# Matrix products that take their columns as two halves in turns, eight columns at a time

## The chip, the cores and the metric

One Trainium2 chip, one of its cores. The time is the device time of one execution of the program in microseconds (us); lower is better. TensorE (PE in the profile) does the matrix products, with its weight loads shown apart as PEld; VectorE (DVE), ScalarE (ACT) and GpSimd (POOL) do the rest, and the SyncE queue (SP) issues the DMAs.

## The reference, cut to what matters

A trunk of two layers on 512 tokens of width 1024, all in float32: a Mamba-2 mixer, a gated MLP, a differential attention mixer, a second gated MLP. The work of interest is that of the big projections, each a product of tokens with a weight matrix:

```python
proj = jnp.einsum('bsd,de->bse', u, w_in)            # 1024 -> 6176, SSM mixer
... jnp.einsum('bse,ed->bsd', y.astype(u.dtype), w_out)   # 2048 -> 1024
qkv = jnp.einsum('bsd,de->bse', u, w_qkv)            # 1024 -> 3072, attention
... jnp.einsum('bse,ed->bsd', out.reshape(b, s, H * ATTN_V_DIM), w_out)  # 1024 -> 1024
h = jnp.einsum('bsd,df->bsf', u, w_up)               # 1024 -> 5632, both MLPs
return jnp.einsum('bsf,fd->bsd', jax.nn.silu(gate) * up, w_down)   # 2816 -> 1024
```

Between them stand RMS norms, short causal convolutions, the chunked state-space recurrence and the attention of 8 heads.

## The kernel before

Activations lie transposed: 128 channels on the partitions, the 512 tokens in the free dimension. A projection is cut into weight units of 8 (or 11) tiles of 128x128. For each unit a DMA brings the float32 weights into `raw`; ScalarE rounds them to fp32r in `w_hi` (L416), VectorE takes the remainder into `w_lo` (L431). The activations are split in the same way into `hn_hi`/`hn_lo`, `y_hi`/`y_lo`, `h_hi`/`h_lo` and `o_hi`/`o_lo`.

The helper `product` (L464 to L470) then issues three fp32r matmuls for each pair of a weight tile and an activation chunk: high weights by high activations (L468), high by low (L469), low by high (L470). All three add into the same PSUM accumulator of 512 columns by 128 partitions, and every matmul is preceded by the load of its own weight tile. The activations are the moving operand: their columns, the tokens, pass through the array one after another. Each operand of `product` is one contiguous stretch of float32 columns along a partition, and so is the accumulator that is written.

`product` is called from `in_unit` (one accumulator of 512 columns for 8 chunks), `first_unit`, `out_halves_pe`, `sout_start`, `aout_step`, and, at the boundaries between phases, from `pair_pe` and `wide_start` with the tokens cut into two parts of 256 columns (`tokens(t)`), so that norms of the first part can start while the second is multiplied. Counted over the program that is 1600 products on 512 columns and 464 on 256 columns, three matmuls each.

All other matmuls are issued elsewhere: float32 products of the recurrence and of the attention (L1080, L1083, L1092, L1111, L1597, L1647), transposes (L1104, L1119, L1607, L1640), norm statistics and broadcasts (L489, L523, L525, L529, L603, L607, L614). Between the units stand waits of the TensorE queue on semaphores (`lo_made` for the weights, `evac` for a free accumulator). The order of all queues is written out by hand in one block per engine. Nothing in the program looks at the order in which the columns of one accumulator were written: VectorE and ScalarE take an accumulator (L1050, for example) only when `unit_done` says that its last matmul has ended.

In the allocation of the program before, the tiles that are moved begin at multiples of 32 bytes in a partition (`hn_lo` at 69984, `hn_hi` at 86368, `h_hi` at 102752, for example), and each accumulator at the start of a PSUM bank of 2048 bytes or 1024 bytes into one.

Of the kernel before, what the change touches and what calls it, by code (L numbers as in the profile page):

```python
# [35 lines left out]
FC = DFF // P  # L36
HU = FC // 2
UW = HU * P
EPS = 1e-6
LAMBDA_INIT = 0.8 - 0.6 * math.exp(-0.3 * 1)  # L40
MASKED = -1e30
# [26 lines left out]
def phases():  # L68
    made, prev = [], None
    for units, chunks, width, kind in (  # L70
            (1 + 6 * NG, 1 + 6 * NG, KC * P, "in"), (2 * KC, KC, KC * P, "out"),
            (2 * FC, 2 * FC, KC * P, "in"), (2 * KC, KC, UW, "out"),
            (3 * NH, 3 * NH, KC * P, "in"), (KC, KC, KC * P, "out"),
            (2 * FC, 2 * FC, KC * P, "in"), (2 * KC, KC, UW, "out")):
        prev = Phase(units, chunks, width, kind, prev)
# [28 lines left out]
def trunk(nc, x_in, w_mix, w_sout, w_up0, w_dn0, w_qkv, w_aout, w_up1, w_dn1, params, lam_in, out):  # L104
    ctx = ExitStack()
    with ctx:
# [4 lines left out]
        def sb(name, shape, dt=F32, scope=ctx):  # L111
            return scope.enter_context(nc.sbuf_tensor(name, shape, dt))
# [4 lines left out]
        x = sb("x", [P, KC, S])  # L117
        raw = sb("raw", [P, 2, UW])
        sb("lead_in", [P, 56])
        w_hi = sb("w_hi", [P, 2, UW], F32R)  # L120
        w_lo = sb("w_lo", [P, 2, UW], F32R)
        sb("lead_out", [P, 72])
# [177 lines left out]
        norm_no, n = {}, 0  # L300
# [155 lines left out]
        def wait_up_bank(pe, ph, j):  # L456
# [4 lines left out]
            else:  # L461
                pe.wait_ge(evac["in"], ph.before["in"] + j - 3)

        def product(acc, slot, c, hi, lo, first, last, weights=None):  # L464

            wh, wl = weights or (w_hi[:, slot, :], w_lo[:, slot, :])
            wh, wl = wh[:, c * P:(c + 1) * P], wl[:, c * P:(c + 1) * P]
            nc.tensor.matmul(acc[:], wh, hi, start=first, stop=False)  # L468
            nc.tensor.matmul(acc[:], wh, lo, start=False, stop=False)  # L469
            return nc.tensor.matmul(acc[:], wl, hi, start=False, stop=last)  # L470

        def in_unit(pe, ph, j, rep):

            pe.wait_ge(lo_made, ph.U0 + j + 1)
            if ph in (UP0, UP1):
                wait_up_bank(pe, ph, j)
                acc = up_acc(ph, rep)
            else:
                wait_bank(pe, ph, j)
                acc = acc_of(ph, rep)  # L480
            for c in range(KC):
                last = product(acc, slot_of(ph, rep), c, hn_hi[:, c, :], hn_lo[:, c, :],
                               c == 0, c == KC - 1)
            last.then_inc(unit_done, 1)
# [79 lines left out]
        def first_unit(pe, j, mid=None):  # L564

            pe.wait_ge(lo_made, j + 1)
            if j in (3, 5, 7):
                pe.wait_ge(evac["in"], {3: 2, 5: 3, 7: 4}[j])
            for c in range(KC):
                last = product(mix_acc(j), slot_of(MIX, j), c, hn_hi[:, c, :], hn_lo[:, c, :], c == 0, c == KC - 1,  # L570
                               halves_of(MIX, j, True))
                if mid is not None and c == mid[0]:
                    mid[1]()
            last.then_inc(unit_done, 1)
# [43 lines left out]
        def pair_pe(pe, ph, b, hi, lo, tiles):  # L618
# [4 lines left out]
            if ph is not AOUT:  # L623
                k0 = tiles
                for s in range(2):
                    u = ph.units - 4 + s
                    pe.wait_ge(lo_made, made_at(ph, u))
                    wait_bank(pe, ph, 2 * END + s)
                    for c in range(tiles):
                        for t in range(2):  # L630
                            last = product(part_acc(ph, t, s), slot_of(ph, u), c, hi[:, c, tokens(t)],
                                           lo[:, c, tokens(t)], c == 0, False)
                    last.then_inc(unit_done, 1)
# [1272 lines left out]
        def _(pool):  # L1906
            n = 0

            def const(ins):
                nonlocal n  # L1910
                ins.then_inc(consts, 1)
                n += 1
# [8 lines left out]
            const(nc.gpsimd.memset(ones[:], 1.0))  # L1921
            const(nc.gpsimd.memset(eps[:], EPS))
            for i, width in enumerate((D, DI // NG, 2 * DH)):
# [241 lines left out]
```

## Time and profile before

| | |
|---|---|
| median of 3 runs | 1435.64 us (1434.94 to 1436.01) |
| profiled execution, device time | 1436.27 us |
| its span, first to last instruction | 1434.5 us |
| PE busy | 1417.3 us, 99% |
| PEld busy | 1192.6 us, 83% |
| DVE busy | 1027.8 us, 72% |
| ACT busy | 621.3 us, 43% |
| POOL busy | 112.9 us, 8% |
| granted TensorE clock, mean | 0.998 of full speed |

The busy time of an engine is the union of the spans of its instructions. Matmul spans overlap each other, since a second one enters the array while the first still drains, so the length of one matmul in the profile (389 ns for 512 columns) is a latency; what a stream of them costs is read from the distance between their starts.

### The profile page before, as it was taken

To read this page: it belongs to the slowest core of one execution; us is meant where nothing else is said; L and a number is where in the kernel's file an instruction comes from. 1 tells how busy PE (TensorE), PEld (TensorE's weight loads), DVE (VectorE), ACT (ScalarE), POOL (GpSimd) and SP (SyncE) were. 2 spreads that over 40 slices of the span, in tenths; PEclk is the share of its full clock that TensorE was granted. 3 is DMA by queue.
4 is the path that set the end of the run, shared out by engine and by line. 5 is a ranking of instruction groups with operands and counts; after the bars stand their busy time and mean duration, and the time that the engine had idled before them with its cause. 6 is when DMAs were issued, how large, how long until landed. Compare 5 with 4: busy or idle time off the path is not lost.

```text
span 1434.5 us, 21763 instructions
## 1 busy us (share of the span) xinstructions
PE 1417.3 (99%) x7506; PEld 1192.6 (83%) x7506; DVE 1027.8 (72%) x1575; ACT 621.3 (43%) x1019; POOL 112.9 (8%) x85
## 2 busy tenths in 40 slices
PE   8999999999999999999999999999999999999997
PEld 6888888888889888888888977777798888888887
DVE  6998889899437888888623677778588888886123
ACT  6656555557334323323323446556563332323221
POOL 0000000000110000000011032321110000000111
PEclk9999999999999999999999999999999999999999
DMA  4433332432231232323233112121212222233331
GB/s 169 176 137 126 142 125 109 138 140 74 89 132 38 96 102 88 102 91 110 101 101 139 31 59 74 59 74 56 89 63 84 92 102 96 94 105 103 101 101 60
DMA packets 37445, 142.34 MB, mean 99 GB/s; under 512 B 4176, under 2 KB 6352, under 8 KB 35344
## 3 DMA queue, kind: packets, MB, share of 16 engines
q1 hardware_dynamic: 37392, 141.63, 28.8%
q8 instruction: 34, 0.56, 0.2%
q14 instruction: 19, 0.16, 0.0%
HBM read 139.38 MB, written 2.23 MB: 99 GB/s over the span
## 4 chain that ended last, share of the span: by engine, by line
PE 94%; DVE 3%; DMA 1%; ACT 1%; issue 1%; SPq 0%; POOL 0%; POOLq 0%; ACTq 0%
PE bank L468 20%; PE bank L470 20%; PE bank L469 20%; PE b_x L468 7%; PE b_x L470 7%; PE b_x L469 7%; PE b_norm L1647 1%; PE b_norm L489 1%; PE b_y L1080 1%; PE b_y L468 1%; PE b_y L470 1%; PE b_y L469 1%; PE b_cb L1607 1%; DVE hn_lo L823 1%; PE b_x L1092 1%; PE b_y L1597 1%
## 5 line engine op out<-in xcount | busy, mean ns | idle before, releaser
L416 ACT ACTIVATE w_hi<-raw 128x1024 fp32r<-128x1024 f32 (+1 forms) x201 | 222.9, 1109 | 406.3 <-PE bank L470 291.1
L431 DVE TENSOR_TENSOR w_lo<-raw,w_hi 128x1024 fp32r<-128x1024 f32 (+1 forms) x181 | 234.1, 1293 | 229.2 <-ACT w_hi L416 229.1
L468 PE MATMUL bank<-hn_hi,w_hi 128*128 128x512 f32 x848 | 335.9, 396 | 2.9 <-DVE hn_lo L804 1.6
L470 PE MATMUL bank<-hn_hi,w_lo 128*128 128x512 f32 x848 | 330.8, 390 | 0.0
L469 PE MATMUL bank<-hn_lo,w_hi 128*128 128x512 f32 x848 | 330.3, 389 | 0.0
L468 PEld LDWEIGHTS bank<-hn_hi,w_hi 128*128 128x128 f32 x848 | 159.3, 188 | 38.1 <-DVE w_lo L431 3.2
L470 PEld LDWEIGHTS bank<-hn_hi,w_lo 128*128 128x128 f32 x848 | 159.2, 188 | 33.9
L469 PEld LDWEIGHTS bank<-hn_lo,w_hi 128*128 128x128 f32 x848 | 159.4, 188 | 32.1
L468 PE MATMUL bank<-h_hi,w_hi 128*128 128x512 f32 (+1 forms) x352 | 127.9, 363 | 0.0
L470 PE MATMUL bank<-h_hi,w_lo 128*128 128x512 f32 (+1 forms) x352 | 127.6, 362 | 0.0
L469 PE MATMUL bank<-h_lo,w_hi 128*128 128x512 f32 (+1 forms) x352 | 127.6, 362 | 0.0
L468 PE MATMUL b_x<-hn_hi,w_hi 128*128 128x512 f32 x320 | 124.6, 389 | 0.0
L469 PE MATMUL b_x<-hn_lo,w_hi 128*128 128x512 f32 x320 | 124.5, 389 | 0.0
L470 PE MATMUL b_x<-hn_hi,w_lo 128*128 128x512 f32 x320 | 124.5, 389 | 0.0
L1064 DVE SCALAR_TENSOR_TENSOR cv_s<-ug_s,par,cv_s 128x512 f32<-128x512 f32 x96 | 72.0, 750 | 6.9 <-DVE cv_s L1064 0.9
L469 PEld LDWEIGHTS bank<-h_lo,w_hi 128*128 128x128 f32 x352 | 66.4, 189 | 10.3
L470 PEld LDWEIGHTS bank<-h_hi,w_lo 128*128 128x128 f32 x352 | 66.4, 189 | 10.3
L468 PEld LDWEIGHTS bank<-h_hi,w_hi 128*128 128x128 f32 x352 | 66.4, 189 | 10.3
L1498 ACT ACTIVATE sg<-cg 128x512 f32<-128x512 f32 x44 | 27.9, 633 | 104.3 <-DVE cg L1064 104.3
L468 PEld LDWEIGHTS b_x<-hn_hi,w_hi 128*128 128x128 f32 x320 | 60.1, 188 | 13.0 <-issue 0.6
L469 PEld LDWEIGHTS b_x<-hn_lo,w_hi 128*128 128x128 f32 x320 | 60.1, 188 | 12.5
L470 PEld LDWEIGHTS b_x<-hn_hi,w_lo 128*128 128x128 f32 x320 | 60.1, 188 | 12.5
(326 smaller groups left out, 2476.7 us busy)
## 6 DMA issues: line engine op xcount, KB each, us to landing
raw<-w_up SPq DMA_DIRECT2D x80, 512.0 KB, 3.2
raw<-w_mix SPq DMA_DIRECT2D x48, 512.0 KB, 3.3
raw<-w_dn SPq DMA_DIRECT2D x32, 704.0 KB, 4.1
raw<-w_qkv SPq DMA_DIRECT2D x20, 512.0 KB, 3.2
acs_bc<-scratch SPq DMA_DIRECT2D x8, 1024.0 KB, 5.7
ecs_bc<-scratch SPq DMA_DIRECT2D x8, 1024.0 KB, 4.7
raw<-w_sout SPq DMA_DIRECT2D x16, 512.0 KB, 3.2
first_raw<-w_up SPq DMA_DIRECT2D x8, 512.0 KB, 6.4
```

Of the source, the lines that this page charges most:

```text
L416: nc.scalar.activation(halves_of(ph, j if own else rep, own or first and j < 4)[0], raw_of(ph, rep, first and j < 4), ACT.Copy).then_inc(h ...
L431: nc.vector.tensor_tensor(lo, raw_of(ph, rep, first), hi.bitcast(F32), ALU.subtract).then_inc(lo_made, 1)
L468: nc.tensor.matmul(acc[:], wh, hi, start=first, stop=False)
L469: nc.tensor.matmul(acc[:], wh, lo, start=False, stop=False)
L470: return nc.tensor.matmul(acc[:], wl, hi, start=False, stop=last)
L489: last = nc.tensor.matmul(b_norm[:, b:b + 1], squares[:, b * P:(b + 1) * P], mean_col[:, mean:mean + 1], start=True, stop=True)
L823: nc.vector.scalar_tensor_tensor(hn_lo[:, m, tokens(t)], x[:, m, tokens(t)], gain(*GAINS[b][1], m), hn_hi[:, m, tokens(t)].bitcast(F32), A ...
L1064: ins = nc.vector.scalar_tensor_tensor(dst, ug[:, t:t + S], col(wcol + t), dst, ALU.mult, ALU.add)
L1080: last = nc.tensor.matmul(dst, xdt[:, c, hh, :], m_t[:, hh, c * P:(c + 1) * P], start=True, stop=c == 0)
L1092: last = nc.tensor.matmul(b_x[:, c // 2, (c % 2) * 2 * P:(c % 2) * 2 * P + 2 * P], btok[:, c, :], xdd[:, c, :, :].rearrange("p h d -> p (h ...
L1498: nc.scalar.activation(sg[:], cg[:], ACT.Silu).then_inc(gate_ready, 1)
L1597: last = nc.tensor.matmul(scores_in[i % 2][:, t, 0:keys], qT[DH * t:DH * t + DH, b1, i * P:(i + 1) * P], kT[DH * t:DH * t + DH, b1, 0:keys ...
```

## The change

`product` gives every operand of its three matmuls another order. `in_turns` splits the columns into two halves (h = 2), and each half into runs of 8 columns (i = 8), and walks run 0 of the first half, run 0 of the second, run 1 of the first, and so on. For 512 columns this is 0 to 7, 256 to 263, 8 to 15, 264 to 271, up to 504 to 511; for the products on 256 columns the two halves are 128 apart. A run is 32 bytes; the next run begins 1024 bytes further on (512 for 256 columns), and the one after that 992 bytes back (480). The accumulator is written in the same order as the moving operand is read, so that every sum lands where it did before. The weight loads, the waits, the queues and all other matmuls stay as they are.

```diff
+RUN = 8
...
+        def in_turns(columns):
+
+            return columns.rearrange("p (h n i) -> p n h i", h=2, i=RUN)
+
         def product(acc, slot, c, hi, lo, first, last, weights=None):
 
             wh, wl = weights or (w_hi[:, slot, :], w_lo[:, slot, :])
             wh, wl = wh[:, c * P:(c + 1) * P], wl[:, c * P:(c + 1) * P]
-            nc.tensor.matmul(acc[:], wh, hi, start=first, stop=False)
-            nc.tensor.matmul(acc[:], wh, lo, start=False, stop=False)
-            return nc.tensor.matmul(acc[:], wl, hi, start=False, stop=last)
+            acc, hi, lo = in_turns(acc), in_turns(hi), in_turns(lo)
+            nc.tensor.matmul(acc, wh, hi, start=first, stop=False)
+            nc.tensor.matmul(acc, wh, lo, start=False, stop=False)
+            return nc.tensor.matmul(acc, wl, hi, start=False, stop=last)
```

## Rows read from the trace of the kernel before

**Rows 1.** Page: span, busy time and share of each engine, granted clock by slices, chain

```profile
span 1434.5 us, 21763 instructions
...
PE 1417.3 (99%) x7506; PEld 1192.6 (83%) x7506; DVE 1027.8 (72%) x1575; ACT 621.3 (43%) x1019; POOL 112.9 (8%) x85
...
PEclk9999999999999999999999999999999999999999
...
PE 94%; DVE 3%; DMA 1%; ACT 1%; issue 1%; SPq 0%; POOL 0%; POOLq 0%; ACTq 0%
```

**Rows 2.** Waits of PE: who waited, for whom, us in total, times, longest

```profile
PE b_cb L558 <- POOL last_row L1916: 3.2, 1, 3.2
PE bank L468 <- DVE hn_lo L804: 1.6, 1, 1.6
PE bank L468 <- DVE w_lo L431: 1.0, 1, 1.0
PE b_cb L1607 <- ACT aT L1691: 0.9, 2, 0.5
```

**Rows 3.** Groups by line and shape: line, tiles, shapes, count, busy us, mean ns

```profile
L468 PE MATMUL bank<-hn_hi,w_hi 128*128 128x512 f32 x848 | 335.9, 396 | 2.9 <-DVE hn_lo L804 1.6 <-DVE w_lo L431 1.0 <-issue 0.2
...
L468 PE MATMUL b_x<-hn_hi,w_hi 128*128 128x512 f32 x320 | 124.6, 389 | 0.0
...
L468 PE MATMUL bank<-h_hi,w_hi 128*128 128x512 f32 x264 | 102.7, 389 | 0.0
...
L468 PE MATMUL bank<-h_hi,w_hi 128*128 128x256 f32 x88 | 25.2, 287 | 0.0
...
L1092 PE MATMUL b_x<-xdd,btok 128*128 128x256 f32 x48 | 11.8, 381 | 0.6 <-DVE xdd L1436 0.6
```

**Rows 4.** Timeline of PE, FFN stage, 512 columns: start us, length us, what

```profile
599.87 0.39 PE L468 MATMUL bank<-hn_hi,w_hi 128*128 128x512 f32 x1
...
600.10 0.39 PE L469 MATMUL bank<-hn_lo,w_hi 128*128 128x512 f32 x1
...
600.33 0.39 PE L470 MATMUL bank<-hn_hi,w_lo 128*128 128x512 f32 x1
...
601.91 0.39 PE L468 MATMUL bank<-hn_hi,w_hi 128*128 128x512 f32 x1
```

**Rows 5.** Timeline of PE at 256 columns, end of the mixer's output projection

```profile
430.78 0.28 PE L468 MATMUL b_x<-y_hi,w_hi 128*128 128x256 f32 x1
...
432.94 0.28 PE L468 MATMUL b_x<-y_hi,w_hi 128*128 128x256 f32 x1
```

**Rows 6.** Timeline of PE from a float32 product into a unit of fp32r products

```profile
102.28 1.46 PE L1092 MATMUL b_x<-xdd,btok 128*128 128x256 f32 x6
...
103.80 0.40 PE L469 MATMUL bank<-hn_lo,w_hi 128*128 128x512 f32 x1
...
105.88 0.39 PE L469 MATMUL bank<-hn_lo,w_hi 128*128 128x512 f32 x1
...
108.83 0.39 PE L470 MATMUL bank<-hn_hi,w_lo 128*128 128x512 f32 x1
```

**Rows 7.** DVE groups by shape: a plain read of PSUM, and one in runs of 64

```profile
L1050 DVE TENSOR_TENSOR ug_f<-bank,r_pre 128x512 f32<-128x512 f32 x40 | 27.5, 687 | 0.0
...
L1436 DVE TENSOR_TENSOR xdt<-b_x,dt_tok 128x512 f32<-128x512 f32 x16 | 10.2, 682 | 0.7 <-PE b_x L1104 0.7
```

**Rows 8.** Stretches: PE, PEld, DVE, ACT, POOL busy us (instructions), clock, DMA share, GB/s

```profile
500.00:750.00 250.00, 250.00 (x1105) 207.01 (x1104) 176.91 (x232) 75.59 (x90) 8.13 (x4) 1.00 0.29 97
1100.00:1290.00 190.00, 190.00 (x840) 157.39 (x839) 157.44 (x214) 57.76 (x71) 0.00 (x0) 1.00 0.29 98
```

## Prediction, made before the change was run

> **What bounds the kernel now.** I read the page first: PE is busy for 99% of the span, the chain that ended last lies on PE for 94%, and the granted clock is full in all 40 slices, that is 2.4 GHz [rows 1]. The waits of PE come to some ten microseconds in all, most of them at the start; the four longest are shown [rows 2]. Then the stretches: over 250 us and over 190 us of the two MLPs PE is never idle, while VectorE is busy for 71% and 83% of the time [rows 8]. So the time is what TensorE's own stream takes. The busy share doesn't say how well that stream runs, since the matmuls overlap. For that I took the distance between starts from the timeline. At 512 columns nine steps lie between 599.87 and 601.91, 226.7 ns each [rows 4]. At 256 columns eighteen steps lie between 430.78 and 432.94, 120.0 ns each [rows 5]. The difference, 106.7 ns for 256 columns, is 0.4167 ns for a column: one column in each cycle of 2.4 GHz. What is left is 13.3 ns for each matmul, whatever its length. So the stream already moves a column in every cycle, and there is no slack under it: whatever the new order costs a column is paid in full.
>
> **How much work the change touches.** Of the 1600 products on 512 columns the largest groups of L468 show 848, 320 and 264; of the 464 on 256 columns the largest shows 88 [rows 3]; the rest follows from the loops. With three matmuls each that is 4800 matmuls of 226.7 ns, 1088.2 us, and 1392 of 120.0 ns, 167.0 us: 1255 us, 87% of the span of 1434.5. They move 4800 x 512 + 1392 x 256 = 2.814 million columns, 1172.5 us at 0.4167 ns, and hold 6192 x 13.3 ns = 82.6 us of the fixed part. In the new order a matmul of 512 columns has 64 runs and 63 jumps between them, one of 256 has 32 runs and 31 jumps: 4800 x 63 + 1392 x 31 = 345,552 jumps.
>
> **Part by part.** The change adds no instruction, no wait and no transfer, and moves none. The weight loads keep their contiguous operand. The number of columns is the same. Three things could have a price.
>
> 1. The jumps of the addresses, on the reading side (SBUF) and on the writing side (PSUM). No matmul in this trace reads or writes in short runs, so the price has to be bounded. The lower end is nothing; below it the stream can't go, as it moves a column in every cycle of the full clock already [rows 1, 4, 5]. Only the fixed part could shrink, and that is a rival below. The nearest rows for a broken pattern are VectorE's: reading PSUM in runs of 64 columns, each with a factor of its own, takes 682 ns for 512 elements, where a plain read of an accumulator takes 687 [rows 7]. That row is no cheap proof, as VectorE moves an element only every 1.3 ns by it and its runs are longer. The upper end is a row of PE itself: float32 products (L1092) have starts (1.46 - 0.38) / 5 = 216 ns apart at 256 columns [rows 6], with 0.38 us as the length of one [rows 3]. That is 0.84 ns for a column, half the rate of fp32r. If the new order were read or written at that rate, 1172.5 us would become some 2345 us or more.
>
> I take nothing. The start of each run lies on a multiple of 32 bytes, since the tiles do and the jumps are multiples of 32; a run therefore fills whole aligned groups of 2, 4 and 8 columns on both sides, and whatever unit up to 32 bytes the memories work in, the number of units touched for a matmul is what it was. Only a unit above 32 bytes, or a stop at every jump, would make it cost.
>
> The page "PSUM — Partial Sum Buffer" of the Trainium skill (section Specifications) speaks against this: it says that any access pattern that isn't contiguous slows matmuls significantly, its lines being 8 bytes. It gives no figure; by it the sum would end anywhere between my estimate and the half-rate case. The page "Advanced Engine Details and Errata" (section Memory Cachelines) says the same and then narrows it: every two consecutive elements should be contiguous, and in SBUF a line of 16 bytes should be hit at least twice. By that reading runs of eight cost nothing. No row here decides between the two.
>
> 2. The set-up of a pattern with three dimensions rather than one, once for each of 6192 matmuls. What a set-up that isn't hidden looks like is seen behind the float32 products: the nine steps from 103.80 to 105.88 take 231.1 ns, the thirteen from 105.88 to 108.83 take 226.9 [rows 6]. So 4.2 ns is the price of a stream whose preparation runs late, and 6192 x 4.2 = 26 us would be the upper end. I take 0: the next matmul's set-up has 120 ns or more of the running one to hide behind [rows 5], and if that cover were gone it is this 26 us that would show.
>
> 3. The readers of the accumulators. They start on `unit_done`, attached to the last matmul, which ends when all columns are written in either order. Cost 0; their cover is the next unit's 24 matmuls, 5.4 us.
>
> **The sum.** The profiled execution took 1436.27 us, span 1434.5 and 1.8 around it. Plus 0 for each part: 1436.3 for such an execution, and 1435.6 as the median, since the profiled one lay 0.6 above it.
>
> **The rivals.**
>
> *A stop at each jump (slower).* If the address generator, the SBUF read or the PSUM write loses one column time at every jump, 345,552 x 0.4167 ns = 144 us come on top: 1580 us. At two column times, one cycle of a 1.2 GHz side, it is 288 us: 1724 us. The place is inside each matmul; it decides from the first cycle lost, since nothing hides it [rows 8]. For it: the stream has no slack at all, one column in every cycle [rows 4, 5]. Against it: aligned runs of eight leave time to fetch ahead. The rule in the PSUM page would be met by this. Chance 10% for one, 7% for two column times.
>
> *Half rate or worse (slower).* If a memory is used in units above 32 bytes, each run wastes the other half of its unit, and the stream goes at the 0.84 ns for a column of the float32 products [rows 6]: 1172.5 us more, some 2610 us. Chance 10%.
>
> *Unhidden set-up (slower).* Part 2 at its upper end: 1462 us; at a fifth of it 5 us, still to be measured. Chance 6%.
>
> *A smaller fixed part (faster).* The 13.3 ns between the columns of two matmuls might depend on where the last column of one and the first of the next lie; the new order ends still at the last column and starts at the first, so I see no reason for it. All of it gone would give 1436 - 83 = 1353 us; a tenth of it is 8 us, 1427 us. Chance 3%.
>
> *The change does not do what it says.* If the order is folded back into a plain one, the time is that of the forecast; this lies in its 64%, and only the experiments behind the result could tell it apart.
>
> **How the numbers follow.** A measurement of this kernel can tell a difference of 0.2%, 2.9 us, from no change. No change 64%, slower 10 + 7 + 10 + 6 = 33%, faster 3%. The likeliest case's own range is 1433 to 1439. The whole range runs from 1433 over the unhidden set-up up to one column time at each jump, 1582: 64 + 6 + 10 = 80%. Two column times, half rate and a gain are left out.
>
> **What would show it.** Right: starts still 226.7 ns apart at 512 columns and 120.0 at 256, in the same stretches; the length of one matmul still 389 and some 287 ns [rows 3]; span within 3 us. A stop at each jump shows as 226.7 + 26.3 = 253 ns and 120.0 + 12.9 = 133 ns (279 and 146 for two), so that the part over 13.3 ns grows with the columns; half rate as some 440 ns; an unhidden set-up as the same few nanoseconds at 512 and at 256. VectorE's and ScalarE's groups shouldn't change in length in any case; in the slow ones they only wait longer for PE. The prediction is wrong if the step at 512 columns moves by more than 0.5 ns.

## The result, and the profile after

The changed kernel takes 1514.56 us (1514.48 to 1516.09, 4 runs) where the kernel before takes 1435.61 (1434.94 to 1436.01): 79 us more, a ratio of 1.0553 with a 95% interval of 1.0535 to 1.0571. The forecast was no change.

| | before | after |
|---|---|---|
| span of the profiled execution | 1434.5 us | 1512.8 us |
| PE busy | 1417.3 us | 1497.6 us |
| PEld busy | 1192.6 us | 1206.9 us |
| DVE busy | 1027.8 us | 1029.4 us |
| ACT busy | 621.3 us | 621.2 us |
| granted TensorE clock, mean | 0.998 | 0.998 |

From the page of the kernel after, the lines that answer to [rows 1]:

```profile
span 1512.8 us, 21763 instructions
...
PE 1497.6 (99%) x7506; PEld 1206.9 (80%) x7506; DVE 1029.4 (68%) x1575; ACT 621.2 (41%) x1019; POOL 111.0 (7%) x85
...
PEclk9999999999999999999999999999999999999999
...
PE 98%; DMA 0%; ACT 0%; DVE 0%; issue 0%; SPq 0%; POOL 0%; POOLq 0%; ACTq 0%
```

The number of instructions is the same, the granted clock is full throughout, which is 2.4 GHz, and VectorE and ScalarE do the same work in the same time. PE has grown by 80 us, and the weight loads (PEld), which overlap it, by 14. PE's waits are as small as before, the largest again the 3.2 us at the start. So the time must lie between the starts of matmuls. The timeline of PE in the same stage as [rows 4], 512 columns:

```profile
639.93 0.40 PE L474 MATMUL bank<-hn_hi,w_hi 128*128 128x512 f32 x1
...
640.17 0.41 PE L475 MATMUL bank<-hn_lo,w_hi 128*128 128x512 f32 x1
...
640.42 0.40 PE L476 MATMUL bank<-hn_hi,w_lo 128*128 128x512 f32 x1
...
642.85 0.40 PE L474 MATMUL b_x<-hn_hi,w_hi 128*128 128x512 f32 x1
```

Twelve steps lie between 639.93 and 642.85: 243.3 ns each, where [rows 4] gave 226.7. At 256 columns (to be read beside [rows 5]) 33 steps lie between these two rows, 123.3 ns each by the unrounded starts, where there were 120.0:

```profile
824.83 0.28 PE L475 MATMUL b_x<-h_lo,w_hi 128*128 128x256 f32 x1
...
828.89 0.29 PE L475 MATMUL bank<-h_lo,w_hi 128*128 128x256 f32 x1
```

4800 x 16.6 + 1392 x 3.3 ns = 84 us; the span grew by 78. Most of the rest is in two places. In the stages with other matmuls between the units of products, a step was up to 231 ns long before the change already [rows 6], and the first seven steps behind such matmuls grew by 11 to 13 ns only. And three stretches of 114 matmuls at 256 columns, one at the head of each projection that follows a boundary between phases, last 14.2 us before and 14.3 after. TensorE waits there for VectorE's splits into `hn_lo`, of which one comes every 1.58 us where twelve matmuls take 1.44 before and 1.48 after, so that a longer step only means less waiting. The groups by shape say the same from another side (they answer to [rows 3]):

```profile
L474 PE MATMUL b_x<-hn_hi,w_hi 128*128 128x512 f32 x320 | 129.8, 406 | 0.0
...
L474 PE MATMUL bank<-h_hi,w_hi 128*128 128x512 f32 x264 | 107.1, 406 | 0.0
...
L474 PE MATMUL bank<-h_hi,w_hi 128*128 128x256 f32 x88 | 25.4, 289 | 0.0
```

One matmul of 512 columns lasts 406 ns in place of 389, 17 more: as much as the step. The time is lost inside the stream of columns, and five times as much at 512 columns as at 256, though there are only twice as many runs. A fixed price for each jump would have given 2 to 1.

For the rest of this document a "step" is the distance between the starts of two matmuls in a stage of one kind, in ns; "at 512" is read from a stretch of 40 us in the middle of the first MLP, "at 256" from its last units. It holds for that stretch; in some orders the same products have another step elsewhere, which is said where it was read. One column time is 0.4167 ns.

### The profile page after: what moved, and what is told of

Same layout as the page of the kernel before. It is cut to its first block, busy times and chain, and to the rows that moved or that the text cites. A ratio compares the mean times of both kernels' runs of the same rounds, so it can differ in the third digit from the quotient of the medians.

```text
span 1512.8 us, 21763 instructions
## 1 busy us (share of the span) xinstructions
PE 1497.6 (99%) x7506; PEld 1206.9 (80%) x7506; DVE 1029.4 (68%) x1575; ACT 621.2 (41%) x1019; POOL 111.0 (7%) x85
## 4 chain that ended last, share of the span: by engine, by line
PE 98%; DMA 0%; ACT 0%; DVE 0%; issue 0%; SPq 0%; POOL 0%; POOLq 0%; ACTq 0%
PE bank L474 21%; PE bank L475 20%; PE bank L476 20%; PE b_x L474 8%; PE b_x L476 8%; PE b_x L475 8%; PE b_y L474 1%; PE b_y L476 1%; PE b_y L475 1%; PE b_norm L1653 1%; PE b_norm L495 1%; PE b_y L1086 1%; PE b_cb L1613 1%; PE b_y L1603 1%; PE b_y L1089 1%; PE b_x L1098 1%
## 5 line engine op out<-in xcount | busy, mean ns | idle before, releaser
L474 PE MATMUL bank<-hn_hi,w_hi 128*128 128x512 f32 x848 | 349.4, 412 | 2.5 <-DVE hn_lo L810 1.2
L476 PE MATMUL bank<-hn_hi,w_lo 128*128 128x512 f32 x848 | 344.5, 406 | 0.0
L475 PE MATMUL bank<-hn_lo,w_hi 128*128 128x512 f32 x848 | 344.4, 406 | 0.0
L474 PE MATMUL bank<-h_hi,w_hi 128*128 128x512 f32 (+1 forms) x352 | 132.5, 376 | 0.0
L475 PE MATMUL bank<-h_lo,w_hi 128*128 128x512 f32 (+1 forms) x352 | 132.3, 376 | 0.0
L476 PE MATMUL bank<-h_hi,w_lo 128*128 128x512 f32 (+1 forms) x352 | 132.2, 376 | 0.0
L474 PE MATMUL b_x<-hn_hi,w_hi 128*128 128x512 f32 x320 | 129.8, 406 | 0.0
L476 PE MATMUL b_x<-hn_hi,w_lo 128*128 128x512 f32 x320 | 129.8, 406 | 0.0
L475 PE MATMUL b_x<-hn_lo,w_hi 128*128 128x512 f32 x320 | 129.8, 406 | 0.0
L474 PEld LDWEIGHTS bank<-h_hi,w_hi 128*128 128x128 f32 x352 | 66.8, 190 | 14.2
L476 PEld LDWEIGHTS bank<-h_hi,w_lo 128*128 128x128 f32 x352 | 66.8, 190 | 14.2
L475 PEld LDWEIGHTS bank<-h_lo,w_hi 128*128 128x128 f32 x352 | 66.7, 189 | 14.3
```

The lines of the kernel that those rows point to most:

```text
L474: nc.tensor.matmul(acc, wh, hi, start=first, stop=False)
L475: nc.tensor.matmul(acc, wh, lo, start=False, stop=False)
L476: return nc.tensor.matmul(acc, wl, hi, start=False, stop=last)
```

## The experiments

### Which side pays, and is it a price for each run?

Four kernels: two other lengths of a run, and the turns on one side only.

```diff
-RUN = 8
+RUN = 16
```

> Runs of 16 columns in place of 8: 32 runs in a matmul of 512 columns, 16 in one of 256. Before the change the starts of matmuls of 512 and 256 columns lay 226.7 and 120.0 ns apart, after it 243.3 and 123.3. Theory A: each run costs one column time (0.4167 ns), and some 10 ns of this vanish in the fixed part of 13.3 ns, so that a step is the larger of (columns + 32) and (columns + runs + 8) column times: 552, 230.0 ns, at 512 and 288, 120.0 ns, at 256. 4800 x 3.3 ns = 16 us, some 1451 us. Theory B: nothing vanishes, the price of a jump depends on its distance, 16.7 / 63 = 0.264 ns at 1024 bytes and 3.3 / 31 = 0.107 ns at 512 bytes: 31 x 0.264 = 8.2 ns at 512 columns, 234.9 ns, and 121.6 ns at 256: some 1474 us.

Measured: 1496.2 us, ratio 1.0417 (1.0399 to 1.0434); steps 240.0 and 120.0 ns. At 256 columns as theory A had it, at 512 columns not: the price is 13.3 ns, where A says 3.3 and B 8.2. Halving the number of runs took away only a fifth of the price of 16.6.

```diff
-RUN = 8
+RUN = 4
```

> Runs of 4 columns: 128 runs in a matmul of 512 columns, 64 in one of 256. Theory A (step = larger of columns + 32 and columns + runs + 8, in column times): 648, 270.0 ns, at 512 and 328, 136.7 ns, at 256; 4800 x 43.3 + 1392 x 16.7 ns = 231 us by the steps, and since the change itself cost 79 us where its steps give 85, some 1650 us. Theory B (0.264 ns for a jump of 1024 bytes, 0.107 for one of 512, nothing vanishes): 260.2 ns and 126.7 ns, some 1595 us. Theory C: a memory works in units of 32 bytes, and half a unit costs as much as a whole one: 1024 columns' time for 512, above 430 ns a step, some 2500 us.

Measured: 1550.8 us, ratio 1.0796 (1.0778 to 1.0814); steps 250.0 and 126.7 ns. Twice the runs added 6.7 ns at 512 columns and 3.4 at 256. A and C fall at both widths, and B, which has the 126.7 at 256 columns, falls at 512, where it says 260.2; there the price is much less than proportional to the runs. A unit of 32 bytes is out: half a unit in place of a whole one costs 6.7 ns, where theory C needs some 200.

```diff
-            acc, hi, lo = in_turns(acc), in_turns(hi), in_turns(lo)
+            acc, hi, lo = acc[:], in_turns(hi), in_turns(lo)
```

> Runs of 8 in turns for the moving operand alone; the accumulator is written as one contiguous stretch. The sums of a column so land in another column of the accumulator; the amount of work is the same. If the whole price is the read side's (SBUF): steps of 243.3 and 123.3 ns, 1514.6 us. If it is the write side's (PSUM): 226.7 and 120.0 ns, 1435.6 us. If each side bears half of it: some 235 ns, 1475 us. If either side alone stops the stream by as much as both: 1514.6 us here and in the run that only writes in turns.

```diff
-            acc, hi, lo = in_turns(acc), in_turns(hi), in_turns(lo)
+            acc = in_turns(acc)
```

> Runs of 8 in turns for the accumulator alone; the moving operand is read as one contiguous stretch. The sums of a column land in another column; the amount of work is the same. If the whole price is the write side's (PSUM): steps of 243.3 and 123.3 ns, 1514.6 us. If it is the read side's (SBUF): 226.7 and 120.0 ns, 1435.6 us. If each bears half: some 235 ns, 1475 us.

Measured: reading in turns alone 1514.7 us, ratio 1.0545 (1.0528 to 1.0563); writing in turns alone 1436.35 us, ratio 0.9998 (0.9989 to 1.0008). The stretch from 600 to 700 us (PE, PEld, DVE, ACT, POOL busy and their instructions, clock, DMA share, GB/s), first with reading in turns, then with writing in turns:

```profile
600.00:700.00 100.00, 100.00 (x413) 77.87 (x412) 76.16 (x103) 28.90 (x36) 0.00 (x0) 1.00 0.25 89
```

```profile
600.00:700.00 100.00, 100.00 (x443) 82.82 (x442) 83.03 (x112) 30.55 (x37) 0.00 (x0) 1.00 0.30 104
```

In 100 us 413 matmuls touch the window in the one and 443 in the other: 243.3 ns against 226.7 a step. This is the cleanest verdict of the study. The whole price is that of reading the moving operand; writing PSUM in this broken order, runs of 32 bytes, is free.

### Does it go away with long runs, and does the distance matter?

```diff
-RUN = 8
+RUN = 32
```

> Runs of 32 columns (128 bytes). The three run lengths tried so far give steps of 576, 584 and 600 column times (0.4167 ns) at 512 columns for 16, 8 and 4 columns a run, where the plain order has 544; at 256 columns 288, 296 and 304 where the plain order has 288. Theory F: a quarter of a column time for each run, and at 512 columns 24 column times on top that do not depend on the length of a run. Then 544 + 24 + 4 = 572, 238 ns, 28 x 0.4167 x 4800 = 56 us by the steps and some 52 us measured: some 1489 us. Theory G: the cost falls away with long runs, since a run of 128 bytes can be fetched ahead: 226.7 ns and 1436.5 us.

Measured: 1478.1 us, ratio 1.0300 (1.0283 to 1.0317); steps 236.7 and 119.0 ns. Near F at 512 columns (238), but at 256 columns the step is 1.0 ns shorter than in plain order, which neither theory had.

```diff
-RUN = 8
+RUN = 128
```

> Runs of 128 columns: in a product of 512 columns four runs, 0 to 127, 256 to 383, 128 to 255, 384 to 511, so three jumps; in a product of 256 columns no jump at all. Theory F (24 column times at 512 columns whatever the run, and a quarter for each run): 569, 237.1 ns, some 1483 us. Theory G (the cost falls away with long runs): 226.7 ns, 1436.5 us. Theory H (the cost comes from the dimensions of the pattern, or from the first jump alone): as F.

Measured: 1436.4 us, ratio 1.0003 (0.9993 to 1.0013), steps 226.7 and 120.0 ns. The pattern still has three dimensions at 512 columns, and three jumps; they cost nothing. So it is not the set-up of such a pattern, nor a single jump. F and H fall, and G holds for runs of 512 bytes, though not for the 128 bytes of the run before.

```diff
-            return columns.rearrange("p (h n i) -> p n h i", h=2, i=RUN)
+            return columns.rearrange("p (h n i) -> p n h i", h=4, i=RUN)
```

> Runs of 8 as in the change, but over the four quarters of the columns in turns instead of the two halves: at 512 columns a jump goes 512 bytes on, the distance that the halves have at 256 columns. Same number of runs and of columns. Theory D (the 24 column times that only the products of 512 columns show belong to jumps of 1024 bytes): 544 + 16 = 560, 233.3 ns, and nothing new at 256 columns; some 1470 us. Theory N (they belong to 512 columns, whatever the distance): 584, 243.3 ns, 1514.6 us.

```diff
-            return columns.rearrange("p (h n i) -> p n h i", h=2, i=RUN)
+            return columns.rearrange("p (n h i) -> p h n i", h=2, i=RUN)
```

> Runs of 8, first all even runs, then all odd ones: 0 to 7, 16 to 23, and so on, then 8 to 15, 24 to 31. As many runs as in the change and the same pattern of three dimensions, but each jump skips 32 bytes only, and the address goes back once. Theory D (the distance of the jumps makes most of the price): at most 560, 233.3 ns, some 1470 us or less. Theory N (the number of runs and of columns make it): 584, 243.3 ns, 1514.6 us. If a memory worked in units above 32 bytes, every unit would be read twice, far apart: above 400 ns and some 2500 us.

Measured: quarters 1453.5 us, ratio 1.0128 (1.0111 to 1.0145), steps 231.1 and 120.0 ns; even-then-odd runs 1458.4 us, 1.0153 (1.0136 to 1.0170), steps 232.4 and 117.8 ns. With the same 64 runs of 8 the price at 512 columns falls from 16.6 to 4.4 and 5.7 ns. Theory N falls. Both steps lie at or under what theory D, the distance, had forecast (at most 233.3 ns); the next run was to test it with everything else as in the change.

### Distance alone, and the weight load beside the stream

The moving operand goes in pairs of runs as in the change, the second a quarter of the columns further on, or not at all (a distance of 0, with 0 in place of `size // 4`); half of the columns are read twice.

```diff
-            return columns.rearrange("p (h n i) -> p n h i", h=2, i=RUN)
+            size = columns.shape[-1]
+            return bass.AP(columns.tensor, columns.offset,
+                           [columns.ap[0], [RUN, size // 2 // RUN], [size // 4, 2], [1, RUN]])
...
-            acc, hi, lo = in_turns(acc), in_turns(hi), in_turns(lo)
+            acc, hi, lo = acc[:], in_turns(hi), in_turns(lo)
```

> The moving operand alone goes in pairs of runs of 8 columns, and the second run of a pair lies a quarter of the columns further on in place of half of them: 512 bytes at 512 columns, 256 bytes at 256. Half of the columns are read twice and the last quarter isn't read, so the products are other ones; as many columns move, in as many runs as in the change. Theory D (the price grows with the distance of a jump): some 555 column times at 512 columns, 231 ns, as the quarters had, and 288, 120.0 ns, at 256: some 1454 us. Theory R (the number of runs alone sets the price, and the quarters were cheap for their other order): 584, 243.3 ns, 1514.6 us.

> The moving operand alone goes in pairs of runs of 8 columns that are one and the same run, read twice: 0 to 7, 0 to 7, 8 to 15, 8 to 15. Only the first half of the columns is read, so the products are other ones; as many columns move. A jump goes 32 bytes back at most. Theory D (distance): no price, 544 and 288 column times, 226.7 and 120.0 ns, 1436 us. Theory R (a price for every run that does not continue the one before): 584 and 296, 1514.6 us.

Measured: 512 bytes apart 1514.8 us, ratio 1.0552 (1.0535 to 1.0570), steps 243.3 and 123.3 ns, those of the change; distance 0 1494.9 us, 1.0412 (1.0395 to 1.0429), steps 240.0 and 120.0. Theory D, which two runs had seemed to bear out, falls: 512 and 1024 bytes cost the same, and even a run that is read again at once costs 13.3 ns a matmul. Theory R falls too, by 3.3 ns: the price isn't quite the same for all.

The next two replace the weight operand with one column of its tile, read 128 times; the second also has the plain order.

```diff
+            wh, wl = (w[:, 0:1].to_broadcast([P, P]) for w in (wh, wl))
             acc, hi, lo = in_turns(acc), in_turns(hi), in_turns(lo)
```

> The change as it is, but each weight load reads one column of its tile 128 times (a step of 0) in place of 128 columns; the products are other ones, the number of loads and of columns in them is the same. Theory W (the stream of the moving operand and the weight load that runs beside it hinder each other in SBUF, and jumps make them meet more often): a load that stays in one place takes the price away or changes it by much: some 544 and 288 column times or fewer, 1436 us or less. Theory O (the moving operand's own reading makes the price): 584 and 296 as in the change, 1514.6 us.

> Plain order of the columns as before the change, with the same weight loads of one column read 128 times; the products are other ones. Theory W (moving operand and weight load hinder each other; the fixed 32 column times, 13.3 ns, are of that kind too): fewer than 544 and 288 column times, down to 512 and 256, which would be 4800 x 13.3 + 1392 x 13.3 = 82 us less, 1354 us. Theory O: 544 and 288, 1436 us.

Measured: turns 1514.05 us, ratio 1.0543 (1.0526 to 1.0561), steps 243.3 and 123.3 ns; plain order 1444.4 us, 1.0067 (1.0049 to 1.0085), steps 231.7 and 113.4 ns. For the turns theory O holds: their steps don't care what the weight load reads. For the plain order both theories are wrong: at 256 columns it gained 6.6 ns, at 512 it lost 5.0 in the first MLP. In the second MLP, with the same tiles, the step is 228.9 ns in the same execution, so it lost 2.2 there. The timeline of the plain order with such loads; thirteen steps lie between the first and the last row, 231.5 ns each:

```profile
559.65 0.39 PE L477 MATMUL bank<-hn_hi,w_lo 128*128 128x512 f32 x1
559.88 0.40 PE L475 MATMUL bank<-hn_hi,w_hi 128*128 128x512 f32 x1
...
562.66 0.40 PE L475 MATMUL bank<-hn_hi,w_hi 128*128 128x512 f32 x1
```

So in plain order what the weight load reads does change the pace of the matmuls. The step of 226.7 ns is no sum of 512 column times and a fixed part of the instruction, as I had taken it.

### Counters, shape, place in memory, alignment

```diff
-            return columns.rearrange("p (h n i) -> p n h i", h=2, i=RUN)
+            return bass.AP(columns.tensor, columns.offset,
+                           [columns.ap[0], [0, columns.shape[-1] // RUN], [1, RUN]])
...
-            acc, hi, lo = in_turns(acc), in_turns(hi), in_turns(lo)
+            acc, hi, lo = acc[:], in_turns(hi), in_turns(lo)
```

> The moving operand alone, and it reads its first run of 8 columns 64 times (32 times at 256 columns), a pattern of two dimensions with a step of 0; the products are other ones, as many columns move. Theory L (every end of a run costs in the counters of the pattern, wherever the next run lies): a price like that of the change, 584 and 296 column times, or 576 and 288 as for runs that were read twice. Theory M (the price is one of fetching other bytes): 544 and 288 column times, 226.7 and 120.0 ns, 1436 us. Theory T (it comes with a middle dimension of two): as M.

Measured: 1384.2 us, ratio 0.9638 (0.9610 to 0.9666), steps 215.8 and 111.6 ns, shorter than any theory allowed. Ten steps lie between these two rows, 216 ns each:

```profile
599.84 0.38 PE L475 MATMUL b_x<-hn_hi,w_hi 128*128 128x512 f32 x1
...
602.00 0.38 PE L476 MATMUL bank<-hn_lo,w_hi 128*128 128x512 f32 x1
```

This is the second finding of weight. Sixty-three ends of a run cost nothing here, so theory L is out: the counters of the pattern aren't what costs. And of the 13.3 ns that stood over 512 column times in plain order, all but 2.5 go away when only the reading of the moving operand is changed. The page "TensorE: Matmul & The Clock Gate" of the Trainium skill (section Wait — 56ns, not 53.3ns?) gives columns at 2.4 GHz and some 2.5 ns for the distance of matmuls back to back, 215.7 ns at 512; this run agrees with 215.8, and the kernel before, with 226.7, does not. At 256 columns the same rule of the Trainium skill gives 109.2 ns, an estimate from that page, and this run has 111.6.

```diff
-            return columns.rearrange("p (h n i) -> p n h i", h=2, i=RUN)
+            return columns.rearrange("p (h n i) -> p n h i", h=8, i=RUN)
```

> Runs of 8 over the eight eighths of the columns in turns, reading and writing alike. As many runs as in the change. Halves gave 584 column times at 512 columns, quarters 554. Theory T (the short middle dimension is dear: what counts is how often two dimensions end at once, 32 times with halves, 16 with quarters, 8 with eighths): below 554, some 547, 228 ns, and some 1442 us. Theory L (runs alone): 554 or more, 1454 us or more.

Measured: 1574.4 us, ratio 1.0963 (1.0931 to 1.0995), the slowest of all. In the first MLP the steps at 512 columns are 263.3 ns on the mean: 16 lie between the first and the last of the first four rows. One in four is short (600.59 to 600.84), the others are 0.27 us. In the mixer's input projection, in the same execution, with the same pattern and the same tiles `hn_hi` and `hn_lo`, 15 steps of 233.3 ns lie between the last two rows:

```profile
599.79 0.44 PE L475 MATMUL bank<-hn_lo,w_hi 128*128 128x512 f32 x1
...
600.59 0.41 PE L475 MATMUL bank<-hn_lo,w_hi 128*128 128x512 f32 x1
600.84 0.44 PE L476 MATMUL bank<-hn_hi,w_lo 128*128 128x512 f32 x1
...
604.00 0.44 PE L476 MATMUL bank<-hn_hi,w_lo 128*128 128x512 f32 x1
```

```profile
73.33 0.40 PE L474 MATMUL bank<-hn_hi,w_hi 128*128 128x512 f32 x1
...
76.83 0.40 PE L474 MATMUL bank<-hn_hi,w_hi 128*128 128x512 f32 x1
```

Theory T falls, and with it every theory that looks at the pattern alone, or at the pattern and the places of the tiles. Through the mixer's input projection the units alternate: the second of the pair behind the state products (L1098) goes at 233.3 ns, the pair after it, on the same activations and the same two weight buffers, at 263. So 30 ns hang on something else, either how the stream got going or what the other engines do meanwhile. The latter can't be all of it: in the plain order with weights of one column the two MLPs, with the same work on every engine, differed by 2.8 ns a step. What decides wasn't found. At 256 columns, though, the step is 113.3 ns, 6.7 less than in plain order.

```diff
-                           [columns.ap[0], [RUN, size // 2 // RUN], [size // 4, 2], [1, RUN]])
+                           [columns.ap[0], [RUN, size // 2 // RUN], [size // 4 + RUN, 2], [1, RUN]])
```

> As the pairs of runs 512 bytes apart (584 column times at 512 columns), but with 544 bytes between them, an odd number of runs, so that a pair no longer lies on the same half of aligned 64, 128 or 256 bytes. Moving operand alone; the products are other ones. Theory B (both runs of a pair fall on the same part of the memory, and that makes them wait): a clear change, down to some 544 to 560, 1436 to 1465 us. Theories L and T (counters): 584, 1514.6 us.

```diff
-RUN = 8
+RUN = 16
...
-        sb("lead_out", [P, 72])
+        sb("lead_out", [P, 80])
```

> Runs of 16 columns in halves, with all tiles behind the weights moved by 32 bytes, so that they begin at multiples of 64 bytes and a run of 64 bytes no longer lies across two aligned groups of 64. Without the shift: 576 and 288 column times, 1496 us. Theory U (a unit of 64 bytes is fetched, and a run across two units costs one more): less, down to 560, 233 ns and some 1466 us. Theories L and T: 576, 1496 us.

Measured: 544 bytes apart 1498.5 us, ratio 1.0434 (1.0403 to 1.0465), steps 240.0 and 120.0 ns; runs of 16 on shifted tiles 1495.8 us, 1.0416 (1.0385 to 1.0446), steps 240.0 and 120.0. An odd number of runs between the two of a pair takes 3.3 of 16.6 ns away, as a distance of 0 did, where theory B needed at least 10; L and T, which had no change, fall too. The shift changes nothing, so aligned units of 64 bytes (theory U) are out. It moves the activations against the weights by 32 bytes as well, and that changes nothing either.

### An order that gains?

Eighths at 256 columns are rounds with one run every 128 bytes. The same at both widths:

```diff
-            return columns.rearrange("p (h n i) -> p n h i", h=2, i=RUN)
+            return columns.rearrange("p (h n i) -> p n h i", n=4, i=RUN)
```

> Runs of 8, four rounds over the columns, each taking one run every 128 bytes: 16 runs a round at 512 columns, 8 at 256. Reading and writing alike. At 256 columns this is the order that the eighths had there, where the steps were 113 ns in place of 120 before the change. Theory K (what counts is how the places that are read spread over the memory beside the weight load, and a step of 128 bytes spreads them well): the same gain at 512 columns, some 220 ns in place of 226.7, so 4800 x 6.7 + 1392 x 6.7 ns = 41 us less, some 1397 us. Theory T (counters: the gain at 256 columns is for short patterns only): at 512 columns between even-then-odd (558 column times) and quarters (554), 231 ns, and 113 ns at 256: some 1447 us.

Measured: 1438.6 us (single runs from 1424.9 to 1440.3), ratio 0.9984 (0.9954 to 1.0014); in the profiled execution of 1438.5 us, steps 230.7 and 113.3 ns. The gain at 256 columns is confirmed. At 512 columns the MLPs have none; the step there is 4 ns longer than in plain order, theory T's number, though not for its reason. But the same execution has a gain elsewhere. In the mixer's input projection 26 steps of 220.0 ns lie between the first two of these rows, and 28 of 230.6 between the last two, on the same tiles:

```profile
65.54 0.38 PE L474 MATMUL bank<-hn_hi,w_hi 128*128 128x512 f32 x1
...
71.26 0.38 PE L476 MATMUL bank<-hn_hi,w_lo 128*128 128x512 f32 x1
...
79.76 0.39 PE L474 MATMUL bank<-hn_hi,w_hi 128*128 128x512 f32 x1
...
86.22 0.40 PE L475 MATMUL bank<-hn_lo,w_hi 128*128 128x512 f32 x1
```

220 ns is what theory K had forecast; the two paces alternate through that projection as with the eighths. Executions of this kernel lie at 1425 to 1428 or at 1438 to 1440, four and six of them, and only one at 1438.5 has a profile. If in the others the 1355 steps at 512 columns of one MLP went at 220.0 ns in place of 230.7, that would be 14 us less, near the 12 between the groups. This is an estimate from the steps above and wasn't seen.

The last kernel takes this order for 256 columns only:

```diff
-            return columns.rearrange("p (h n i) -> p n h i", h=2, i=RUN)
+            if columns.shape[-1] == S:
+                return columns[:]
+            return columns.rearrange("p (h n i) -> p n h i", n=4, i=RUN)
```

> Products of 512 columns in plain order as before the change; those of 256 columns in runs of 8, four rounds of eight runs 128 bytes apart, reading and writing alike. If the steps seen with that order at 256 columns hold beside plain ones at 512: 113.3 and 226.7 ns, 1392 x 6.7 = 9.3 us less, some 1427 us. If the boundaries between phases, where most products of 256 columns are, wait for VectorE's splits instead: the steps are shorter, and PE waits longer for hn_lo and w_lo, between 1427 and 1436 us.

Measured: 1430.35 us (1429.39 to 1432.13, 6 runs) against 1436.04, ratio 0.9964 (0.9952 to 0.9976). It is 0.4% faster than the kernel before, clear of the noise, by 5.7 us of the 9.3 that the steps would give. The stretches of 114 matmuls behind the boundaries keep most of the rest: they last 14.1 us where they took 14.2, with eleven steps over 150 ns in place of six, as they wait for VectorE's splits, still one every 1.58 us. That is the second case of the expectation. At 256 columns 37 steps lie between these rows, 113.3 ns each by the unrounded starts:

```profile
774.73 0.28 PE L478 MATMUL b_x<-h_hi,w_lo 128*128 128x256 f32 x1
...
778.92 0.28 PE L476 MATMUL bank<-h_hi,w_hi 128*128 128x256 f32 x1
```

### All orders side by side

| order of the moving operand | step at 512 | step at 256 | time, us |
|---|---|---|---|
| one run of 8 again and again | 215.8 | 111.6 | 1384.2 |
| plain | 226.7 | 120.0 | 1435.6 |
| halves, runs of 128 | 226.7 | 120.0 (plain there) | 1436.4 |
| one run of 8 every 128 bytes | 230.7, and 220.0 in parts of the mixer | 113.3 | 1438.6 |
| plain, weights one column | 231.7, and 228.9 in the second MLP | 113.4 | 1444.4 |
| quarters, runs of 8 | 231.1 | 120.0 | 1453.5 |
| even, then odd runs of 8 | 232.4, and 233.3 in the second MLP | 117.8 | 1458.4 |
| halves, runs of 32 | 236.7 | 119.0 | 1478.1 |
| runs of 8, each read twice | 240.0 | 120.0 | 1494.9 |
| halves, runs of 16 (with or without shift) | 240.0 | 120.0 | 1496.2 |
| pairs of runs of 8, 544 bytes apart | 240.0 | 120.0 | 1498.5 |
| **halves, runs of 8 (the change)** | 243.3 | 123.3 | 1514.6 |
| pairs of runs of 8, 512 bytes apart | 243.3 | 123.3 | 1514.8 |
| halves, runs of 4 | 250.0 | 126.7 | 1550.8 |
| eighths, runs of 8 | 263.3 in the MLPs, 233.3 in parts of the mixer | 113.3 | 1574.4 |

## Why the prediction was wrong

**What bounds the kernel: right.** The loss went into the time of TensorE's stream nearly one to one. 4800 and 1392 matmuls, 16.6 and 3.3 ns more a step, give 84 us against the 79 measured. Only at three boundaries, where VectorE's splits set the pace, did a wait take up about 1 us of it.

**Part 1, the jumps at 0: wrong on the read side, right on the write side.** This is the step that failed. The write side's 0 is measured (1436.35 us). The page "PSUM — Partial Sum Buffer" of the Trainium skill (section Specifications) says that a pattern that isn't contiguous slows matmuls significantly; for the accumulator, with runs of 8, no price can be seen here. On the read side I argued that aligned runs of 32 bytes touch as many units of memory as the plain order, and that units above 32 bytes would be needed for a price. It isn't so: the jumps on the read side, which the sum had at 0, cost 16.6 ns a matmul at 512 columns and 3.3 at 256, 79 us in all, and reading alone in the new order takes 1514.7 us. Nor does the argument by units hold. A run that is read again and again is free and a run that is read twice costs 13.3 ns, so neither the number of units nor the ends of runs decide. The same holds against the reading that I drew from "Advanced Engine Details and Errata" of the Trainium skill (section Memory Cachelines), two hits on each SBUF line of 16 bytes: runs of 4 are four hits, and cost 23.3 ns.

**Part 2, the set-up at 0: right.** Three dimensions on the read side cost nothing with runs of 128, nor on the write side with runs of 8.

**Part 3, the readers of the accumulators at 0: right.** DVE's busy time moved by 1.6 us.

**The fixed part: the premise was wrong.** I split 226.7 and 120.0 ns into one column for each cycle and 13.3 ns for the instruction, "whatever its length", and took from it that the stream had no slack and that every lost cycle would be paid in full. That two widths fit a straight line proved nothing about what the intercept is. With one run read again and again 10.9 of the 13.3 ns go away at 512 columns and 8.4 at 256. That part belongs to the plain order, and so another order can lower it as well as raise it. The rival that I gave 3% for want of a reason, a smaller fixed part, exists: 6.7 ns at 256 columns are real and bring 0.4% in the last kernel. The prediction looked for it between the last column of one matmul and the first of the next; it comes with the order of reading in between.

**The rivals.** "A stop at each jump" came nearest, with the right sign and place: inside each matmul, on the read side. Its term was 345,552 jumps of one column time, 144 us; measured were 79. By size the term is 0.26 ns for a jump at 512 columns (16.6 / 63) and 0.11 at 256 (3.3 / 31), and the runs of 4 and 16 show that it is no price for a jump at all: a fourth of the runs lowers the price at 512 columns only from 23.3 to 13.3 ns. Half rate and unhidden set-up are excluded. The time lies inside the range only because the range reached to a rival, and that is luck: no case had a mechanism that gives 79 us.

**Signs named beforehand.** The step at 512 columns moved by 16.6 ns where 0.5 was to prove the forecast wrong; the length of one matmul by 17; the engines' groups not at all. The proposed test "does the part over 13.3 ns grow with the columns" gave the first hint: it grew five times for twice the columns.

**What stays open.** The cause within the read side isn't settled. Shown is where it isn't: writing PSUM, set-up, ends of runs as such, distances of 512 against 1024 bytes, aligned units of 32 or 64 bytes. Shown is also that the pace depends on the distance by little (3.3 ns between 512 and 544 bytes); in plain order on what the weight load reads (226.7 against 231.7, 120.0 against 113.4); and in some orders it takes two values on the same tiles in the same execution (eighths: 263 against 233 ns; one run every 128 bytes: 230.7 against 220.0). Neither a fixed price for a pattern nor the place of the tiles can give that; how the stream got going before it, or traffic of other engines beside it, might. A conflict of two streams of reads in SBUF would fit the plain order; it doesn't explain that the turns keep 243.3 ns with either kind of weight load. A theory of banks for the moving operand alone would have to explain why a run read twice is dear and one read 64 times is free. I have none that fits all rows of the table. Tiles moved against the weights by amounts other than 32 bytes, the same stretch started behind another kind of matmul, and a profile of the order with 128 bytes at 1425 to 1428 us weren't tried.

## What to carry to other kernels

Where TensorE's stream is the bound, leave the moving operand in one contiguous stretch, or in runs of at least 512 bytes, unless the order has been timed at the very shape and place: runs of 16 to 128 bytes cost 4 to 23 ns on a matmul of 512 columns in the MLPs, once 37, and one such order gained 7 or lost 4 in different stretches of one execution. So read the steps of every stage, not of one. A broken order in the accumulator is free at runs of 32 bytes, so where columns have to be permuted and either side would do, permute them on the way out. And an intercept found from two widths is not yet a cost of the instruction: ask what a run without the suspected traffic would leave of it.

## What the runs showed of the hardware

- The moving operand's order sets the step of an fp32r matmul of 512 columns anywhere from 215.8 to 263.3 ns at a full clock of 2.4 GHz, and 11 ns of the 226.7 of the plain order go away when one run is read again and again.
- Short orders can be faster than plain ones: one run of 32 bytes every 128 bytes takes 113.3 ns at 256 columns against 120.0; at 512 it takes 230.7 against 226.7 in the MLPs and 220.0 in parts of the mixer.
- The pace can depend on what the weight load beside it reads: in plain order, a load of one column read 128 times moved the step by -6.6 ns at 256 columns and by +5.0 at 512 in the first MLP, by +2.2 in the second.
- One pattern on the same tiles can run at two steady paces in one execution, 233.3 or 263.3 ns for eighths, 220.0 or 230.7 for one run every 128 bytes. What decides between them wasn't found.
- An fp32r accumulator of 512 columns written in runs of 32 bytes from two halves in turns costs nothing: 226.7 ns a step, 1436.35 us.
- Two distances of one pattern, 512 and 1024 bytes, gave the same steps; 0 and 544 bytes gave 3.3 ns less.
